# Reading the moving operand of every weight product alternately from two halves, and joining the hi and lo products in most panels

## The reference

```python
# first block (16 heads of 128)
a = rms_norm(h, norm_mix);  q, k, v = split(a @ w_qkv)           # 2048 x 6144
z = q @ k.T * 128**-0.5                                           # stick breaking attention
A = where(mask, exp(log_sigmoid(z) + sum over later keys of -softplus(z)), 0)
h = h + (A @ v) @ w_o
h = h + square(relu(rms_norm(h, norm_mlp) @ w1)) @ w2             # 2048 x 8192, 8192 x 2048
x = rms_norm(h, final_norm)
# second block, 16 meta tokens ahead of the 256
u, gb, gc, v, ga, gbr = split(rms_norm(x) @ w_in)                 # 2048 x 12288
y_a = (trailing means of u over 2, 4, 8, 16 tokens, minus u) @ pool_w * pool_scale
y_b = (gb * causal_conv(gc * v, 3 taps)) @ conv_out_w
h = x + (sigmoid(ga + b) * y_a + sigmoid(gbr + b) * y_b) @ w_o2
gate, up = split(rms_norm(h) @ w_gate_up)                         # 2048 x 11264
h = h + (silu(gate) * up) @ w_down                                # 5632 x 2048
out = rms_norm(h)[:, 16:]
```

## Time and profile before

| | |
|---|---|
| median of 3 runs | 2559.87 us (2559.19 to 2560.02) |
| the profiled execution's own time | 2559.02 us |
| its span in the trace | 2557.3 us |
| PE busy | 2548.0 us (100%) |
| DVE, ACT, POOL busy | 1579.5, 1153.8, 142.3 us (62, 45, 6%) |
| DMA | 485.64 MB, mean 190 GB/s |
| mean granted TensorE clock | 0.999 |

### The profile page before, as it was taken

How to read it: one execution, slowest core, us unless ns; L and a number is a source line. 1 busy time by engine, 2 the same in 40 slices (tenths; PEclk the granted TensorE clock), 3 DMA queues, 4 the chain that set the end, 5 groups by cost and what they waited for, 6 DMA issues and landing times.

```text
span 2557.3 us, 47399 instructions
## 1 busy us (share of the span) xinstructions
PE 2548.0 (100%) x19871; PEld 2463.6 (96%) x19871; DVE 1579.5 (62%) x1343; ACT 1153.8 (45%) x1126; POOL 142.3 (6%) x87
## 2 busy tenths in 40 slices
PE   9999999999999999999999999999999999999998
PEld 9999999999999999999999999999999889998997
DVE  6577766655556556787754786666655555555555
ACT  5455545434434444544533344444444434443444
POOL 0000100000000000000200530000000000000001
PEclk9999999999999999999999999999999999999999
DMA  8555555555565566555555556655565555555563
GB/s 263 186 165 165 165 177 187 198 190 190 197 197 191 190 195 197 188 189 182 198 183 184 182 194 203 205 197 184 182 197 196 182 191 190 196 197 190 190 212 132
DMA packets 243977, 485.64 MB, mean 190 GB/s; under 512 B 7728, under 2 KB 8944, under 8 KB 243696
## 3 DMA queue, kind: packets, MB, share of 16 engines
q1 hardware_dynamic: 243520, 483.12, 57.6%
q10 hardware_dynamic: 320, 0.53, 0.1%
HBM read 481.53 MB, written 2.10 MB: 189 GB/s over the span
## 4 chain that ended last, share of the span: by engine, by line
PE 99%; DVE 0%; issue 0%; POOL 0%; ACT 0%; DVEq 0%; POOLq 0%; ACTq 0%
PE ps L1430 48%; PE ps L1438 24%; PE ps L1401 8%; PE ps L1361 8%; PE ps L1407 4%; PE ps L1372 4%; PE ps L1486 0%; PE ps L1540 0%; PE ps L1452 0%; PE ps L1474 0%; PE ps L1423 0%; PE ps L1545 0%; PE ps L1523 0%; PE ps L1292 0%; PE ps L1477 0%
## 5 line engine op out<-in xcount | busy, mean ns | idle before, releaser
L801 DVE TENSOR_TENSOR wlo<-raw,whi 128x1024 fp32r<-128x1024 f32 x900 | 1139.5, 1275 | 929.9 <-ACT whi L590 928.6
L590 ACT ACTIVATE whi<-raw 128x1024 fp32r<-128x1024 f32 x900 | 949.5, 1060 | 1319.4 <-PE ps L1438 1013.9
L1430 PE MATMUL ps<-b_buf,whi 128*128 128x256 f32 x5734 | 713.0, 277 | 0.5 <-DVE za L1019 0.5
L1430 PEld LDWEIGHTS ps<-b_buf,whi 128*128 128x128 f32 x5734 | 681.0, 188 | 1.1 <-DVE za L1019 0.7
L1438 PE MATMUL ps<-b_buf,wlo 128*128 128x256 f32 x2880 | 387.0, 277 | 0.0
L1438 PEld LDWEIGHTS ps<-b_buf,wlo 128*128 128x128 f32 x2880 | 354.9, 188 | 0.0
L1430 PE MATMUL ps<-a_buf,whi 128*128 128x258 f32 (+4 forms) x2560 | 330.8, 282 | 0.0
L1430 PE MATMUL ps<-c_buf,whi 128*128 128x256 f32 x2542 | 316.7, 277 | 0.0
L1430 PEld LDWEIGHTS ps<-a_buf,whi 128*128 128x128 f32 x2560 | 315.8, 188 | 0.3
L1430 PEld LDWEIGHTS ps<-c_buf,whi 128*128 128x128 f32 x2542 | 302.5, 188 | 0.2
L1438 PE MATMUL ps<-a_buf,wlo 128*128 128x258 f32 (+4 forms) x1280 | 179.8, 283 | 0.1
(11 more groups left out here) (208 smaller groups left out, 1254.9 us busy)
## 6 DMA issues: line engine op xcount, KB each, us to landing
raw<-in_mlp_w_dram SPq DMA_DIRECT2D x128, 1024.0 KB, 5.4
raw<-in_w_in_dram SPq DMA_DIRECT2D x96, 1024.0 KB, 5.1
raw<-in_w_gate_up_dram SPq DMA_DIRECT2D x88, 1024.0 KB, 5.1
raw<-in_sb_w_qkv_dram SPq DMA_DIRECT2D x44, 1024.0 KB, 5.1
raw<-in_w_down_dram SPq DMA_DIRECT2D x44, 1024.0 KB, 5.0
raw<-in_sb_w_o_dram SPq DMA_DIRECT2D x16, 1024.0 KB, 5.0
raw<-in_conv_out_w_dram SPq DMA_DIRECT2D x16, 1024.0 KB, 5.0
raw<-in_w_o_dram SPq DMA_DIRECT2D x16, 1024.0 KB, 5.1
```

What stands on the lines that cost most here:

```text
L590: act.activation(whi[:, unit_of(n, u)], raw[:, n % RAW, u * UK:(u + 1) * UK, :], ACT.Copy).then_inc(w_hi, 1)
L801: dve.tensor_tensor(wlo[:, s], raw[:, n % RAW, u * UK:(u + 1) * UK, :], cast(whi[:, s]), ALU.subtract).then_inc(w_lo, 1)
L1430: pe.matmul(outs[j], whi[:, s, kt, j * P:(j + 1) * P], part[:, x, tok], start=first and kt == 0 and part is hi and (alone or j % 2 == 0), ...
```

## The change

All products with weights take their moving operand by turns from its two halves (new `by_turns` and `parts_by_turns`). The output in PSUM stays contiguous, so the tokens (or, where weights move, the weight columns) lie in PSUM in the turned order, and the reads out of PSUM (`narrow`, `wide`, `token_bank`) turn them back. For kinds with token rows the halves are the two halves of 512 weight columns, for wide kinds two halves of 129 to 136 tokens.

The paired form is used in relu2, add, res2, co, resb, gate and up as well, so in all panels but q, k, res (w_o), pw and the wide and token-row kinds; the table RUNS and the form with 4 or 5 joint products go. A paired chunk now has its own 16 products of 512, then its 16 of 256. These panels get a `cross_out` on ACT and a cross step on DVE. `row_sum` and the q step are done as two instructions of half the size.

```diff
-PER_RUN = UNITS * UK * JT
-RUNS = ((15, 15, 18, 16), (16, 15, 15, 18))
...
-            add("w1_0", 1, [Panel("relu2", "w1", ..., needs="w_o", pairs=(4, 5, 0, 0)[g])
+            add("w1_0", 1, [Panel("relu2", "w1", ..., needs="w_o", pairs=True)
...
-                                     needs="w_o") for h in range(2)], ("relu2",))
+                                     needs="w_o", pairs=True) for h in range(2)], ("relu2",))
...
-    loop2("wo2", "resb", "w_o2", 0, "C", "co")
+    loop2("wo2", "resb", "w_o2", 0, "C", "co", pairs=True)
...
+        def by_turns(row):
+            return row.rearrange("p (a n) -> p n a", a=2)
+        def parts_by_turns(rows_):
+            return rows_.rearrange("p c (a n) -> p c n a", a=2)
+        def in_halves(cols):
+            return cols.rearrange("p b (a n) -> p b a n", a=2)
         def narrow(half):
-            return ps[:, 4 * half:4 * half + 2, :].rearrange("p b (t n) -> p (b t) n", t=2)
+            return ps[:, 4 * half:4 * half + 2, :].rearrange("p b (t n a) -> p (b t) a n", t=2, a=2)
+        def token_bank(bank):
+            return ps[:, bank, :].rearrange("p (n a) -> p a n", a=2)
...
                 if kind == "q":
-                    last = dve.scalar_tensor_tensor(out=full[:], in0=n, scalar=QK_SCALE, in1=r, ...)
+                    for a in range(2):
+                        last = dve.scalar_tensor_tensor(out=lay(full[:])[:, :, a, :], in0=n[:, :, a, :], ...)
...
-                dve.tensor_tensor(y_tok[:, :, cols], y_tok[:, :, cols], ps[:, 4 * half:4 * half + MT, :],
-                                  ALU.add).then_inc(full_ready, 1)
+                for m in range(MT):
+                    y = two_halves(y_tok[:, m, cols])
+                    last = dve.tensor_tensor(y, y, token_bank(4 * half + m), ALU.add)
+                last.then_inc(full_ready, 1)
...
-            def paired_chunk(p, c, k):
+            def paired_chunk(p, c, half):
...
+                for u in range(UNITS):
+                    pe.wait_ge(w_hi, cnt.at("chunk") * UNITS + (u + 1))
+                    for kt in range(UK):
+                        for j in range(JT):
+                            pe.matmul(ps[:, 4 * half + j, :].rearrange("p (c n a) -> p c n a", c=2, a=2),
+                                      whi[:, unit_of(n, u), kt, j * P:(j + 1) * P],
+                                      parts_by_turns(buf[:, :, p.tile0 + c * KT + u * UK + kt, tok]),
+                                      start=c == 0 and u == 0 and kt == 0, stop=False, skip_group_check=True)
...
-                                    pe.matmul(ps[:, 4 * half + m, :], part[:, x, toks[m]], whi[:, s, kt, :],
+                                    pe.matmul(ps[:, 4 * half + m, :], part[:, x, toks[m]], by_turns(whi[:, s, kt, :]),
...
-                            for kt, x, j in products[len(joint):]:
-                                pe.matmul(outs[j], whi[:, s, kt, j * P:(j + 1) * P], part[:, x, tok],
+                            for kt, x, j in products:
+                                pe.matmul(outs[j], whi[:, s, kt, j * P:(j + 1) * P], by_turns(part[:, x, tok]),
```

More of the change, by code:

```diff
@@ L98, with __init__ @@
 class Panel:
-    def __init__(self, kind, weight, row0, col, chunks=CH, tile0=0, src=None, needs=None, pairs=0):
+    def __init__(self, kind, weight, row0, col, chunks=CH, tile0=0, src=None, needs=None, pairs=False):
         self.kind, self.weight, self.row0, self.col = kind, weight, row0, col
@@ L216, in make_stages @@
         if f == 0:
-            add("w1_0", 1, [Panel("relu2", "w1", 0, lambda i, g=g: g * PW, src="C", needs="w_o", pairs=(4, 5, 0, 0)[g])
+            add("w1_0", 1, [Panel("relu2", "w1", 0, lambda i, g=g: g * PW, src="C", needs="w_o", pairs=True)
                             for g in range(4)],
@@ L646, in cross_out @@
                     act.wait_ge(low_done, cnt.at("low"))
[L647 to L650, removed]
+                    act.activation(in_halves(full[:]), turned(half, 1), ACT.Copy).then_inc(act_done, 1)
             def evac(p, j):
@@ L972, in evac @@
                 dve.wait_ge(pool_done, cnt.at("pool"))
[L973 removed]
+                n, lay = narrow(half), in_halves
                 r = rows(rr[:, M:TW], T)
[L975 removed]
+                if p.pairs:
                     step(dve.tensor_tensor(in_halves(full[:]), turned(half, 0), in_halves(full[:]), ALU.add))
[L977 to L980, removed]
+                    n, lay = full[:], lambda cols: cols
                 if kind == "q":
[L982 to L983 removed]
+                    for a in range(2):
+                        last = dve.scalar_tensor_tensor(out=lay(full[:])[:, :, a, :], in0=n[:, :, a, :],
+                                                        scalar=QK_SCALE, in1=lay(r)[:, :, a, :],
+                                                        op0=ALU.mult, op1=ALU.mult)
                 elif kind == "k":
[L985 removed]
+                    last = dve.tensor_tensor(lay(full[:]), n, lay(r), ALU.mult)
                 elif kind == "v":
                     for m in range(MT):
[L988 to L989 removed]
+                        last = dve.tensor_scalar(full[:].rearrange("p (m t) n -> p m t n", m=MT)[:, m],
+                                                 token_bank(4 * half + m), stat[:, 6 + m:7 + m], None, ALU.mult)
                 elif kind == "add":
@@ L1005, in evac @@
                     lo = WIDE[kind]
-                    step(dve.tensor_tensor(U[:, :, lo:TW], wide(half, lo), rows(rr[:, lo:TW], TW - lo), ALU.mult))
+                    step(dve.tensor_tensor(in_halves(U[:, :, lo:TW]), wide(half, lo),
+                                           in_halves(rows(rr[:, lo:TW], TW - lo)), ALU.mult))
                     src, bufs, w = U, [S1, S2], 1
@@ L1412, in chunk @@
                         tok = slice(lo_col, TW) if wide_ else slice(off, off + T)
-                        alone = wide_ or p.kind in FOUR
                         if wide_:
                             outs = [ps[:, 4 * half + j, lo_col:TW] for j in range(JT)]
-                        elif alone:
-                            outs = [ps[:, 4 * half + j, 0:T] for j in range(JT)]
                         else:
@@ L1420, in chunk @@
                         products = [(kt, x, j) for kt, x in kts for j in range(JT)]
-                        joint = products[:p.pairs] if first else []
-                        for kt, x, j in joint:
-                            pe.matmul(ps[:, 4 * half + j, :].rearrange("p (a n) -> p a n", a=2),
-                                      whi[:, s, kt, j * P:(j + 1) * P], buf[:, :, x, tok], start=kt == 0, stop=False,
-                                      skip_group_check=True)
                         for part in (hi, lo):
```

88 lines of the change are left out of this document (34 added, 54 removed).

## The result

The changed kernel takes **2460.4 us** (median of four runs, 2458.57 to 2460.8) against 2559.88 us: a ratio of 0.961, 95% interval 0.9594 to 0.9627. The forecast was 2462 us, range 2452 to 2482. Its profiled execution took 2460.64 us with a span of 2458.9 us, at a mean granted clock of 0.999; that is 98.4 us less span than the kernel before.

What follows compares the result with a forecast made beforehand. PE bounds the kernel, so time follows the distance between product starts. From 2559.0 us, five steps gaining 101.9 us and costs of 4.6 us gave 2461.7, forecast as 2462 us, range 2452 to 2482.

Steps and rivals of the forecast that it cites:

- Step 1: Relu2, add, res2, co, resb, gate and up, 240 chunks: plain to paired, 5.240 us a chunk, gains 54.2 us.
- Step 2: q and k, 32 chunks, and w_o, 16 chunks: read by turns at 5.34 us a chunk, gaining 9.8 and 5.0 us.
- Step 3: Wide panels by turns: 5.34 us scaled by columns, 5.38 at 258 to 5.67 at 272, gaining 16.5 us.
- Step 4: Token rows, 60 chunks in dn and v: 5.19 us a chunk by turns, gaining 11.0 and 5.4, together 16.4 us.
- Step 5: The 48 already paired chunks of ga, gb, gbr and co: new order of 16 and 16 at the same rate, gaining nothing.
- The norm of u: Start of stage u: PE would wait 2.3 us for DVE, whose fold of sums had 0.8 us slack before.
- pw's wait: Stage pw: what its 4 chunks gain is lost waiting for POOL and DVE, and up to 0.7 us more.
- The weight loads of the values: Values in attention: 0.1 to 0.2 us lost in three of four groups, 0.6 us with their other waits.
- New distances that gain nothing: Wide halves or token rows: one kind gains nothing, 2478 us, chance 0.12; both fail, 2495 us, chance 0.04.
- streams of 256 that fall into a slower state: q, k and w_o keep their time: 2477 us, chance 0.06; short runs in paired chunks too: 2492 us, chance 0.03.
- the cross step on the path: Each of 60 new cross steps holds PE for DVE's 1.22 us: 73 us more, 2535 us, chance 0.05.
- the slower rival: Token rows: weights read by turns 1 KB apart cost an access per element, 0.433 us a product, 2775 us; chance 0.04.

## Why the prediction was right

- **The bound.** PE's starts, not its busy time, carried the whole sum, and each rate read in one stage of before held in the others.
- **Step 1, paired panels.** 54.2 predicted, 54.3 measured; both plain rates vanished at once. Pairing without turns gives nothing, so the step was right only because the earlier trace rows already had both together.
- **Step 2, q, k and w_o.** The term was mis-sized by its rate: 0.1117 us and not the 0.1113 of a run of 16. That is 0.02 us a chunk. q and k still gained 0.5 more than forecast, since the first panel lost less than the 1.0 us that I had put down for DMA.
- **Step 3, wide panels.** The scaling by columns failed: 258 and 260 columns cost what 256 do, as a floor lies above all three. That made gc and vv 0.7 and u1 to u3 1.1 us better than forecast. The step says 52 chunks, but its sum has 48, rightly: the other four are pw's, which stand among the costs.
- **Step 4, token rows.** 0.2158 for the 0.2163 that I took. The halves 256 values apart read as those 128 apart; 4 values are far enough.
- **Step 5, the order of a chunk.** Nothing, shown by the run with uneven runs.
- **The costs.** No PE wait names the cross step, and its 1219 ns did not change. The norm of u waited 1.8 us for the 2.3 forecast; with full clock u0 is 0.6 us longer than before, where I had 0.9. The step that failed is that a wait of PE costs its own length: in the profile of the result 1.65 us of low clock stood behind it, and with the wait removed most of it came back one panel later. pw's wait grew by 0.6 us as feared, but the four chunks kept 0.2 of their gain. The weight loads of the values waited 1.3 us in three groups, 0.4 each, a row that before had none in the list. PE itself lost less: in the first group its first value product starts 172.87 − 171.81 = 1.06 us behind the start of the last four v products, before 180.26 − 179.33 = 0.93, with v products 0.06 longer in sum, so some 0.2 us later, as forecast. v's gain less these waits is 0.2 us short of the forecast.
- **Not in the sum:** the first weight product comes at 8.34 us, before at 7.24. Over the profiles of the twelve kernels with the change or parts of it that start lies between 7.41 and 8.34, set by when the inputs land.
- **The rivals.** New distances that gain nothing, streams of 256 that fall into a slower state, and the cross step on the path: none appeared. The price named in the slower rival, an access per element at 0.433 us, is real: 0.453 at step 2. Its condition was wrong. In the terms of model M, what costs is a stream that leaves its 16 bytes after one value, and turns between two distant halves walked value by value don't make it do so. The Trainium skill, in Advanced Engine Details and Errata, section SBUF Cachelines, has the 16 bytes and the penalty for an access to another line each time; step 2, where each line is hit twice in a row, already doubles the time here, and turns between two lines, another one at each access, are the fastest read, where it names that case as slow.

## What to carry to other kernels

Where PE is the bound, take the distance between starts of products per stage and per reading pattern before counting products: here the order in which the same values are read is worth 3% and the joint form alone nothing. Read a 4-byte moving operand by turns from two regions at least 16 bytes apart, each walked forward value by value: a step of 2 in a single pass doubled the time, and a step of 4 did so even by turns from two halves. A product of fewer than some 260 columns with 128 weight columns gained nothing by being narrower, down to the 128 tried here, so join such products where two share their weights, and read the joint one by turns.

## What the runs showed of the hardware

- A product of 512 4-byte columns: 0.216 us by turns (4 to 256 values apart), 0.227 to 0.231 straight or 2 apart, 0.281 by turns from four quarters, 0.328 in pairs by turns, 0.450 to 0.461 at steps where each stream takes one value of 16 bytes.
- Products with 128 weight columns, each with its load, follow each other at 0.1117 us, whether 128, 192, 224, 240, 256, 258 or 260 columns move; with 64 weight columns a product of 192 takes 0.0825 us.
- After a wait of 1.8 to 2.0 us PE ran its next products at the low level of the clock in two of eight profiles (a granted clock of 0.53 over 16 products in the one shown above), in the others at 1.00.
- Plain products of 256 have two rates (0.113 and 0.118 us) in the kernel before; read by turns they have one. What switches between the two stays open: no run looked for it.
